# Second block of a two-block kernel on one NeuronCore: hyena's chain among the gate units, attention by pairs of heads

## What is computed

```python
def mix(h, p, rope, kv_ext):                       # second block
    z = h @ p["w_in"]                              # q, k, v, z_hy, gates
    q, k = apply_rope(rmsnorm(q)), apply_rope(rmsnorm(k))
    k, v = concat([k, k_ctx]), concat([v, v_ctx])  # 256 own keys + 256 of the context
    attn = gqa_blocks(q, k, v)                     # 8 heads of 64, softmax over 512 keys
    hy = hyena(z_hy, conv_w, conv_b, kf, skip)     # two orders: y = x_o * (fftconv(y, kf_o) + skip*y)
    g_attn, g_hy = jnp.split(gates, 2, axis=-1)
    merged = sigmoid(g_attn) * (attn @ w_attn_out) + sigmoid(g_hy) * (hy @ w_hy_out)
    return merged @ w_out
x = x + g1 * mix(...)
x = x + g2 * peer(modulate(rmsnorm(x)), ...)       # per token 128 rows of u_tab, 128 rows of v_tab
```

## Time and profile before

| | before |
|---|---|
| median of 3 runs | 1783.85 us (1782.99 to 1785.73) |
| span of the profiled execution | 1783.7 us |
| PE busy | 1504.7 us, 84% of the span |
| DVE busy | 882.4 us, 49% |
| ACT busy | 319.5 us, 18% |
| POOL busy | 505.8 us, 28% |

### The profile page before, as it was taken

The page is one execution under the profiler, slowest core; times in us unless marked ns, Lnnn a source line. Parts: engine busy times, 40 slices in busy tenths (PEclk is TensorE's granted clock), DMA queues, the critical chain, the costliest instruction groups (busy, mean ns, idle before and its releaser), DMA issues.

```text
span 1783.7 us, 18187 instructions
## 1 busy us (share of the span) xinstructions
PE 1504.7 (84%) x6234; PEld 833.2 (47%) x6234; DVE 882.4 (49%) x2004; ACT 319.5 (18%) x647; POOL 505.8 (28%) x540
## 2 busy tenths in 40 slices
PE   8989999999999999999999987576767676767667
PEld 6856554434343434478757776232322222322222
DVE  3986143222232323452153697766665657562744
ACT  3113222111010101301230111321111111120110
POOL 3000000000000000000000254757676767676764
PEclk9999989999999999999999987788788888888889
DMA  9686746999999999942302296999898999999997
GB/s 332 238 296 236 291 149 262 424 429 427 428 429 429 428 428 429 390 143 108 129 1 83 76 379 242 394 354 409 334 396 338 400 342 390 356 379 352 397 355 278
DMA packets 135278, 565.40 MB, mean 317 GB/s; under 512 B 11497, under 2 KB 17430, under 8 KB 122732
## 3 DMA queue, kind: packets, MB, share of 16 engines
q1 hardware_dynamic: 60588, 295.66, 41.4%
q0 software_dynamic: 74416, 268.84, 39.3%
q10 hardware_dynamic: 208, 0.09, 0.0%
HBM read 563.49 MB, written 1.06 MB: 317 GB/s over the span
## 4 chain that ended last, share of the span: by engine, by line
PE 77%; issue 10%; DMA 5%; DVE 4%; POOL 2%; ACT 2%; another core or an unknown queue 0%; ACTq 0%; DVEq 0%; POOLq 0%
PE psum L409 53%; PE psum L1018 21%; DMA ring<-in_peer_v_dram,attnT 2%; POOL ring L1164 2%; DMA ring<-in_peer_u_dram,attnT 1%; DMA dft<-in_peer_v_dram,attnT 1%; PE psum L760 0%; DVE arena L1650 0%; PE psum L766 0%; PE psum L417 0%; DMA tok<-in_peer_u_dram,attnT 0%; DVE spec L1653 0%; DVE ring L1974 0%; DVE scratch L1973 0%; DVE ring L1972 0%
## 5 line engine op out<-in xcount | busy, mean ns | idle before, releaser
L1018 PE MATMUL psum<-ring,arena 128*128 128x512 f32 x772 | 380.4, 643 | 182.3 <-issue 91.1
L409 PE MATMUL psum<-ring,arena 128*64 128x512 f32 (+1 forms) x1552 | 343.8, 594 | 1.4 <-DVE arena L1833 1.4
L1018 PEld LDWEIGHTS psum<-ring,arena 128*128 128x128 f32 x772 | 155.8, 204 | 403.2 <-issue 317.3
L1164 POOL DMA_INDIRECT dft<-in_peer_u_dram,attnT x10 | 9.5, 950 | 1002.7 <-DVE attnT L2098 998.6
L2128 DVE CUSTOM_DVE_ANT_0 scratch<-ring,psum 128x1024 f32<-128x1024 f32 x216 | 254.8, 1218 | 65.3 <-DMA ring<-in_peer_u_dram,attnT 48.7
L409 PE MATMUL psum<-actT,ring 128*128 128x256 f32 (+1 forms) x1424 | 267.7, 349 | 22.1 <-issue 18.6
L409 PEld LDWEIGHTS psum<-actT,ring 128*128 128x128 f32 x1424 | 238.8, 197 | 51.4 <-issue 28.3
L1164 POOL DMA_INDIRECT ring<-in_peer_u_dram,attnT x216 | 205.5, 951 | 159.8 <-issue 64.5
L1164 POOL DMA_INDIRECT ring<-in_peer_v_dram,attnT x218 | 211.2, 969 | 72.5 <-issue 62.5
L409 PEld LDWEIGHTS psum<-ring,arena 128*64 128x64 f32 (+1 forms) x1552 | 110.4, 137 | 219.4 <-issue 206.0
L1451 ACT ACTIVATE arena<-ident,attnT 128x128 f32<-128x128 f32 x226 | 80.5, 395 | 393.1 <-PE psum L1018 149.9
...
## 6 DMA issues: line engine op xcount, KB each, us to landing
...
```

The source lines that it names most:

```text
L409: return nc.tensor.matmul(o, lhsT, rhs, start=(k == 0), stop=(k == n - 1))
L1018: last = nc.tensor.matmul(psum[:, 4 + 2 * t + n, :], diag[:, i, :], rowbufs[b][:, n * 512:(n + 1) * 512], start=first, stop=final)
L1164: pool.indirect_dma_start(out=rowbufs[b], out_offset=None, in_=tab, in_offset=bass.IndirectOffsetOnAxis(ap=rowid[:, j // 4, k:k + 1], axis ...
```

## The change

- **Hyena first.** The eight gate units are no longer two blocks of four; hyena's steps of both orders stand between single gate units, before the attention, on banks 0 to 3. The gate units use banks 4 to 7. `hy_rows(0)` follows the transposes of q and k directly and waits for the first two channel blocks alone. DVE does all of hyena before the first maximum.
- **Attention by pairs.** The unit is now a pair of heads (2p, 2p+1) of one token half, first all four pairs of token half 0, then those of half 1. The two scores stand together; one DVE maximum reads both banks (128x1024); the eight transposes stand together; `pv2` interleaves the two heads, matmul by matmul, so that neighbours write rows 0 to 63 and 64 to 127 of the same bank. `pT2` has four buffers instead of two.
- **Projections among the units.** Hyena's output projection for token half 0 stands ahead of the loop, that of half 1's first column half in four pieces of four matmuls within it, and attention's for token half 0 behind pairs 5 and 6. Before, all five groups stood behind the attention. `merge_half` writes over the gate and adds once both branches are there.
- **Ring slots.** Slot 5 holds no gate weights any more, as hyena needs it from its start; the pieces behind it move one slot on, and the row buffers of PEER with them.
- **ACT** loads the table for the square root right after attention's last copy, by an extra one-column operation.

The diff, cut to its core (`gate_unit2`, `hy_spectrum` and `hy_back` do what their forerunners did):

```diff
-        pT2 = scratch[:, 0, :].rearrange("p (u c) -> p u c", c=512)
+        pT2 = scratch[:, :, :].rearrange("p a (u c) -> p (a u) c", c=512)
...
-        rowbufs += [ring[:, 3, r * D:(r + 1) * D] for r in range(4)] + [ring[:, 4, r * D:(r + 1) * D] for r in range(4)]
+        rowbufs += [ring[:, 4, r * D:(r + 1) * D] for r in range(4)] + [ring[:, 0, r * D:(r + 1) * D] for r in range(4)]
...
-        rowbufs += [ring[:, s_, r * D:(r + 1) * D] for s_ in (2, 5, 1, 0) for r in range(4)]
+        rowbufs += [ring[:, s_, r * D:(r + 1) * D] for s_ in (3, 5, 2, 1) for r in range(4)]
...
-                   ("g00", kpiece(w_in2, g2), 5), ("g01", kpiece(w_in2, g2 + 512), 0),
-                   ("g10", kpiece(w_in2, g2 + D), 1), ("g11", kpiece(w_in2, g2 + D + 512), 2),
-                   ("o0", A["w_attn_out_2"][0].rearrange("(k p) n -> p k n", p=P), 3),
-                   ("o1", A["w_hy_out_2"][0].rearrange("(k p) n -> p k n", p=P), 4),
-                   ("wo0", kpiece(A["w_out_2"][0], 0), 0), ("wo1", kpiece(A["w_out_2"][0], 512), 1),
-                   ("pq0", kpiece(A["peer_wq_2"][0], 0), 2), ("pq1", kpiece(A["peer_wq_2"][0], 512), 5),
-                   ("pq3", kpiece(A["peer_wq_2"][0], 1536), 0), ("pq2", kpiece(A["peer_wq_2"][0], 1024), 1)]
+                   ("g00", kpiece(w_in2, g2), 0), ("g01", kpiece(w_in2, g2 + 512), 1),
+                   ("g10", kpiece(w_in2, g2 + D), 2), ("g11", kpiece(w_in2, g2 + D + 512), 3),
+                   ("o0", A["w_attn_out_2"][0].rearrange("(k p) n -> p k n", p=P), 4),
+                   ("o1", A["w_hy_out_2"][0].rearrange("(k p) n -> p k n", p=P), 0),
+                   ("wo0", kpiece(A["w_out_2"][0], 0), 1), ("wo1", kpiece(A["w_out_2"][0], 512), 2),
+                   ("pq0", kpiece(A["peer_wq_2"][0], 0), 3), ("pq1", kpiece(A["peer_wq_2"][0], 512), 5),
+                   ("pq3", kpiece(A["peer_wq_2"][0], 1536), 1), ("pq2", kpiece(A["peer_wq_2"][0], 1024), 2)]
...
+            def gate_unit2(br, i, among=None):
+                landed(place2, f"g{br}{i // 2}")
+                w = pview(place2, f"g{br}{i // 2}")
+                b = bank(f"bg{br}{i}", among)
+                for c in range(2):
+                    m = (2 * (i % 2) + c) * P
+                    for k in range(KD):
+                        last = mm(psum[:, b, c * T:(c + 1) * T], w[:, k, m:m + P], actT[:, k, :], k, KD)
+                last.then_inc(bank_full[b], 1)
...
+            def hy_rows(o):
+                src = (zs[:, 0:4, :], y1T)[o]
+                pe.wait_ge(ev(("short_done", "y1_ready")[o]), (2, 1)[o])
+                for t in range(NT):
+                    b = bank(f"vt{o}{t}", (0, 1, 2, 3))
...
-            gate_units2(0)
...
-            gate_units2(1, (4, 5, 6, 7))
+            hy_rows(0)
+            gate_unit2(0, 0, (4, 5, 6, 7))
+            hy_spectrum(0)
+            gate_unit2(0, 1, (4, 5, 6, 7))
+            gate_unit2(0, 2, (4, 5, 6, 7))
+            hy_back(0)
+            gate_unit2(0, 3, (4, 5, 6, 7))
+            hy_rows(1)
+            gate_unit2(1, 0, (4, 5, 6, 7))
+            hy_spectrum(1)
+            gate_unit2(1, 1, (4, 5, 6, 7))
+            gate_unit2(1, 2, (4, 5, 6, 7))
+            hy_back(1)
+            pairs = [(p, t) for t in range(NT) for p in range(HEADS // 2)]
+            def score2(i):
+                p, t = pairs[i]
+                for r in range(2):
+                    b = bank(f"sc{2 * i + r}", (3, 0, 1, 2))
+                    score(b, 0, 2 * p + r, t, 0, 2 * T).then_inc(bank_full[b], 1)
+            def pt2(i):
+                for u in (2 * i, 2 * i + 1):
+                    pe.wait_ge(ev("p2_ready"), u + 1)
+                    b = bank(f"qt{u}", (4, 5))
+                    for kc in range(4):
+                        last = nc.tensor.transpose(psum[:, b, kc * P:(kc + 1) * P], prob2[:, u % 4, kc * P:(kc + 1) * P], ident[:, :])
+                    last.then_inc(bank_full[b], 1)
+            def pv2(i):
+                p, t = pairs[i]
+                for u in (2 * i, 2 * i + 1):
+                    emptied(pe, f"qt{u}")
+                if p == 0:
+                    bank(f"pw{t}", (7,))
+                b = groups[f"pw{t}"][0]
+                for kc in range(4):
+                    for r in range(2):
+                        u, g = 2 * i + r, (p // 2) * HD
+                        last = mm(psum[r * HD:(r + 1) * HD, b, p * P:(p + 1) * P], vtok[:, kc, g:g + HD],
+                                  pT2[:, u % 4, kc * P:(kc + 1) * P], kc, 4)
+                if p == HEADS // 2 - 1:
+                    last.then_inc(bank_full[b], 1)
+            def mixed_half(br, t, u, among=None, chunks=(0, 1, 2, 3)):
+                wo = ring[:, place2[f"o{br}"][0], :].rearrange("p (k n) -> p k n", k=KC)
+                if chunks[0] == 0:
+                    bank(f"bo{br}{t}{u}", among)
+                b = groups[f"bo{br}{t}{u}"][0]
+                for c in chunks:
+                    m = (4 * u + c) * P
+                    for k in range(KC):
+                        last = mm(psum[:, b, c * P:(c + 1) * P], wo[:, k, m:m + P], (attnT, hyoT)[br][:, k, t * P:(t + 1) * P], k, KC)
+                if chunks[-1] == 3:
+                    last.then_inc(bank_full[b], 1)
...
-            units = [(h, t) for h in range(HEADS) for t in range(NT)]
-            def score2(u):
-                h, t = units[u]
-                b = bank(f"sc{u}", (0, 1, 2, 3, 4))
-                score(b, 0, h, t, 0, 2 * T).then_inc(bank_full[b], 1)
...
-            hy_parts = {0: (hy_rows, 0), 1: (hy_spectrum, 0, 0), 3: (hy_spectrum, 0, 1), 6: (hy_back, 0, 0), 7: (hy_back, 0, 1),
-                        9: (hy_rows, 1), 10: (hy_spectrum, 1, 0), 12: (hy_spectrum, 1, 1), 15: (hy_back, 1, 0)}
-            for u in range(3):
-                score2(u)
-            for u in range(16):
-                if u + 3 < 16:
-                    score2(u + 3)
-                if u in hy_parts:
-                    hy_parts[u][0](*hy_parts[u][1:])
-                pt2(u)
-                if u:
-                    pv2(u - 1)
-            pv2(15)
-            hy_back(1, 1)
...
-            landed(place2, "o0")
-            for i in range(4):
-                emptied(pe, f"pw{i}")
-            mixed_half(0, 0, 0)
-            mixed_half(0, 0, 1)
+            score2(0)
+            gate_unit2(1, 3, (4, 5, 6, 7))
+            score2(1)
             landed(place2, "o1")
             pe.wait_ge(ev("hy_ready"), 1)
-            mixed_half(1, 0, 0)
-            mixed_half(1, 0, 1)
-            mixed_half(0, 1, 0)
+            mixed_half(1, 0, 0, (6,))
+            mixed_half(1, 0, 1, (7,))
+            for i in range(len(pairs)):
+                if i + 2 < len(pairs):
+                    score2(i + 2)
+                pt2(i)
+                if i:
+                    pv2(i - 1)
+                if i < 4:
+                    mixed_half(1, 1, 0, (6,), (i,))
+                if i == 5:
+                    landed(place2, "o0")
+                    emptied(pe, "pw0")
+                    mixed_half(0, 0, 0, (6,))
+                if i == 6:
+                    mixed_half(0, 0, 1, (0,))
+            pv2(len(pairs) - 1)
+            everyday.append((7, 1, 2, 3, 4, 5, 6, 0))
             pe.wait_ge(ev("bmerged"), 1)
             out_unit_rows(place2, "b", 0, 0)
             out_unit_rows(place2, "b", 0, 1)
-            mixed_half(0, 1, 1)
+            emptied(pe, "pw1")
+            mixed_half(0, 1, 0)
...
-            mixed_half(1, 1, 0)
+            mixed_half(0, 1, 1)
...
+                if nm == "pq1":
+                    filled("I11")
...
+            hy_rows(0)
+            gate_out2(0)
+            hy_spectrum(0)
+            gate_out2(1)
+            gate_out2(2)
+            gate_out2(3)
+            hy_rows(1)
+            hy_spectrum(1)
+            full(act, "bg13")
+            for i in (1, 2, 0, 3):
+                copy_out(f"bg1{i}", pair(actT, i), func=ACT.Sigmoid)
+            exp_units(0)
+            for i in range(HEADS):
+                if i + 1 < HEADS:
+                    exp_units(i + 1)
+                for u in (2 * i, 2 * i + 1):
+                    copy_out(f"qt{u}", pT2[:, u % 4, :])
+                if i == 4:
+                    copy_out("pw0", attnT[:, :, 0:P])
+            copy_out("pw1", attnT[:, :, P:T])
+            a(nc.scalar.activation(stat("warm", 1), epscol[:, 0:1], ACT.Sqrt))
...
+            def unit_max(i):
+                us = slice(2 * i, 2 * i + 2)
+                full(dve, f"sc{2 * i}")
+                full(dve, f"sc{2 * i + 1}")
+                b = groups[f"sc{2 * i}"][0]
+                v(V.tensor_reduce(stat("m2", 16)[:, us], psum[:, b:b + 2, :], AX.X, ALU.max))
+                v(V.tensor_scalar(stat("nm2", 16)[:, us], stat("m2", 16)[:, us], -HD ** -0.5, None, ALU.mult), "nmax")
+            def unit_norm(i):
+                us = slice(2 * i, 2 * i + 2)
+                for u in (2 * i, 2 * i + 1):
+                    emptied(dve, f"sc{u}")
```

(31 more changed lines are left out.)

154 lines of the change are left out of this document (36 added, 118 removed).

## The result

| | before | with the change |
|---|---|---|
| median | 1783.53 us (1782.99 to 1785.73) | 1764.86 us (1760.72 to 1767.66) |
| ratio | | 0.9889 [0.9873, 0.9905] |
| span of the profiled execution | 1783.7 us | 1758.9 us |
| hy0, the first hyena projection, starts | 774.71 | 772.34 |
| first group times w_out starts | 974.67 | 951.77 |

The forecast was 1766.8 us. The stage was to become 17.1 us shorter and became 20.5. Another 2.4 us of the profiled run lie ahead of the stage, in code that the change doesn't touch (a stretch at the lower clock near 256 us lasted 3.4 us in this execution, and some 13.6 in that of before), so they are not the change's. The medians differ by 18.7 us. Since the runs of one kernel spread by up to 7 us, I measure the parts by the length of the stage, and the kernels by their medians.

What follows compares the result with a forecast made beforehand. PE's program bounds the kernel up to the first gather, the DMA engines' pace afterwards. Gains less new waits and clock loss sum to 17.1 us off the 1783.7 span; with 0.15 to the median, 1766.8 us, range 1761.6 to 1773.5.

Steps and rivals of the forecast that it cites:

- pv: Attention's pv by pairs: column halves run side by side, 1.2 us a pair, saving 6.7 us (bounds 8.3 and 1.1).
- the clock: After the 4.7 us idle at hyena's first transposes, PE at half speed for 6.8 us; cost 2.6 (bounds 0 and 3.4).
- wait (b): New wait at the first score, whose bank holds hyena's last group, which DVE must read first; 1.4 us.
- wait (c): New wait in the attention loop: DVE's merge_half(1,1,0) runs ahead of the normalising that PE's turn 4 needs; about 0.8 us.
- wait (a): New wait at hy_rows(0): its bank 1 holds k's transposes, which DVE reads only behind the short convolution; 4.7 us.
- Scores by pairs: In attention, two heads' scores on different row halves run side by side; saves 7.0 us (bounds 0 and 7.0).
- Transposes: In attention, eight transposes together instead of four, taking 1.02 us a pair; saves 1.3 us in all.
- rival 3: Something unmoving bounds what follows the w_out product, so half the gain could go: 1775 us; chance 0.05.
- Rival 4: Clock stays at its lower level through the attention, the array being used by halves: kernel up to 1817 us; chance 0.03.
- Waits that go: PE's waits for DVE and ACT before the second gate block and in the attention vanish: 10.0 us.
- Projections: Five output projection groups still precede the w_out product; within the loop they add a turn of shape, about -0.5 us.

Runs made afterwards that it cites:

- the third experiment: The changed kernel with the second score of six of the eight pairs placed behind the eight transposes; 1698.68 us, 0.9926 of the kernel before.
- the first experiment: The changed kernel with hyena's bank rotation turned, so its first transposes avoid the bank of k's transposes; 1685.09 us, 0.9846 of the kernel before.
- the last run: The changed kernel without its three waits, with hyena's projection (1,1,0) and its merge moved behind the w_out product; 1681.15 us, 0.9817 of the kernel before.

## Why the prediction was right, and where it wasn't

**The total.** 20.5 us instead of 17.1. By its own terms: pv 1.4 more (8 x (1.2 - 1.03)), the clock 1.2 more, wait (b) 0.15 and wait (c) 0.3 more, wait (a) 0.1 less; 2.9 of the 3.4. The other 0.5 wasn't traced.

**Held.** Scores by pairs 1.06 each (1.07 taken; the third experiment gives 7.5 us for six pairs with its waits). Transposes 1.02 (1.02). Wait (a) 4.83 (4.7), with its cause, the bank, shown by turning the rotation. Waits (b) 1.25 (1.4) and (c) 0.52 (0.8); both went when their order was changed. What follows the w_out product moved as one block: 38.48 against 38.76 us to the first gather (without the extra table load 38.86), and 768.7 against 770.3 behind it; rival 3 fell. Rival 4 fell as well: PEclk is 1.00 from 872 to the w_out product.

**pv: the mechanism right, the size too cautious.** The pair's pv was bounded by 1.0 and 1.9 and taken at 1.2, for fear that the weight loads, four times as dense as in the earlier trace rows, would spoil the overlap. It is 1.03, the lower bound: the sixteen records of a pair cost what eight did. Beside its 1.9 the prediction put a rule of the Trainium skill, "TensorE: Matmul & The Clock Gate", section "Part 3: Packing small matmuls", by which a weight load overlaps matmuls in flight only if its rows differ. The trace disagrees with the 1.9, at 128 columns as at 512. The same section's table gives a speedup of 2.38 for three column tiles, so that its rule alone did not carry the step to 1.9. The earlier trace rows was the row to go by entirely.

**The clock: a size that isn't fixed.** The term was 2.6, from 6.8 us at half speed as in the earlier trace rows. In the profiled run it was 3.4 us with a loss of 1.4 (the first experiment); on the second chip 6.8 us beside the same wait, with a loss of 2.1. A single execution's length was taken for a constant, and it wasn't asked how much of a stretch would lie in the wait itself.

**The attribution failed, though the sum came out.** Two steps of the prediction are wrong in kind. First, "Waits that go" gave the 10.0 us of waits, and 2.1 of clock, to hyena's move among the gate units. Done alone, that move makes the kernel 0.16% slower (interval 0.02 to 0.30), and with the new wait (a) taken away as well, 0.35% faster. The waits at the attention's begin (0.71 and 1.76 there, for ACT's gate sigmoids and DVE's normalising) stay, and a half-clock stretch of their own stands behind them. The earlier trace rows had named the first of them, 0.71 for ACT's `actT`, but the prediction covered hyena's latencies only. Second, "Projections" was priced by its turns of shape only, -0.5. The two groups ahead of the loop are the cover for ACT's sigmoids, table load and first exponentials, and the two behind pairs 5 and 6 that for DVE's last normalisings; all behind the attention instead, they leave 5.4 us of waits and 3.1 us in the stretch at the lower clock. The four pieces within the loop cover next to nothing: with them moved away one wait of 0.30 us appears (the last run). The prediction listed a cover for every step of hyena, but for the first exponentials it looked only at the loop in its steady state ("2.9" of ACT against "3.3" of PE a pair), not at its start, where the sigmoids and the table load stand ahead of the first exponential (908.64 to 912.43). Pairs alone don't gain either (1.0005): against their 16.5 us (7.1 of scores, 1.3 of transposes, 8.1 of pv) stand 10.7 us more of waits, and 18.1 busy us at the lower clock where before has 5.05, as hyena's latencies lose the attention work that covered them.

So the parts aren't a sum. Pairs shorten PE's work by 16 us, hyena's move takes DVE's long products out from under that shorter work, and the projections fill its start. Hyena's move and pairs are each worth nothing or little alone, and with the projections 20.5 us; the projections' move alone was not run. The total was right because the sum counted the waits left in the final order. In part that was luck: this order holds a cover for the attention's begin that the prediction never worked out, and its two cautious terms, pv and the clock, erred to the same side.
